# Two spacer tensors in SBUF grow by 32 bytes each, under the operands' high and low parts

## What is computed

```python
# first block
mod = silu(c) @ w_ada + b_ada                      # 1024 x 6144, one row
h = layer_norm(x) * (1 + sc1) + sh1
proj = h @ w_in                                    # gated conv (31 taps), pooling, two gates
mix = (sigmoid(gate_a) * ya + sigmoid(gate_b) * yb) @ w_out
x = layer_norm(ALPHA * x + g1 * mix)
up = causal_dwconv(h2 @ w_up, w_dw_f)              # 3 taps, 2 x 2816 channels
x = layer_norm(ALPHA * x + g2 * ((gelu(gt) * v) @ w_down))
# second block, layer 0: gated delta rule, 8 heads; layer 1: block attention, 8 heads
h = layer_norm_2(a * h + mixer(h))
h = layer_norm_2(a * h + (silu(h @ w1) * (h @ w3)) @ w2)   # 2816 channels, in both layers
```

## Time and profile before

| | us |
|---|---|
| median of three executions | 1171.5 |
| lowest, highest | 1166.29, 1176.5 |
| the profiled execution | 1169.08 |
| its span, from first to last instruction | 1167.3 |
| TensorE busy in it | 1109.0 |
| VectorE busy | 807.5 |
| ScalarE busy | 614.9 |

### The profile page before, as it was taken

The page is one execution under the profiler, slowest core; times in us unless marked ns, Lnnn a source line. Parts: engine busy times, 40 slices in busy tenths (PEclk is TensorE's granted clock), DMA queues, the critical chain, the costliest instruction groups (busy, mean ns, idle before and its releaser), DMA issues.

```text
span 1167.3 us, 20553 instructions
## 1 busy us (share of the span) xinstructions
PE 1109.0 (95%) x8544; PEld 1068.4 (92%) x8544; DVE 807.5 (69%) x1360; ACT 614.9 (53%) x1028; POOL 3.3 (0%) x13
## 2 busy tenths in 40 slices
PE   7998989999999998879989999999999999999997
PEld 7998878899999987679989999999999799999996
DVE  7988489877878787586666755555589656555555
ACT  5567444555555648742454554545455545545453
POOL 0000000000000000000000000000000000000000
PEclk9999999999999998989989999999999999999998
DMA  9985247257666523234224266565536332665620
GB/s 377 418 314 179 74 145 279 95 175 246 229 223 210 180 76 113 61 102 146 73 73 143 70 205 198 183 197 184 160 120 201 130 128 91 217 198 181 197 75 37
DMA packets 58557, 195.60 MB, mean 168 GB/s; under 512 B 10848, under 2 KB 11232, under 8 KB 58208
## 3 DMA queue, kind: packets, MB, share of 16 engines
q1 hardware_dynamic: 58464, 194.28, 49.1%
HBM read 192.94 MB, written 1.31 MB: 166 GB/s over the span
## 4 chain that ended last, share of the span: by engine, by line
PE 73%; DVE 17%; ACT 7%; issue 2%; SPq 1%; DMA 0%; POOL 0%; ACTq 0%; DVEq 0%; POOLq 0%
PE ps L512 61%; DVE lo L1475 4%; PE ps L725 3%; ACT hi L1008 2%; DVE raw L1462 2%; PE ps L610 2%; PE ps L519 2%; DVE B L1484 1%; PE ps L531 1%; DVE ev L1713 1%; DVE st L1492 1%; PE ps L507 1%; DVE ev L1710 1%; DVE B L1788 1%; DVE B L1497 1%
## 5 line engine op out<-in xcount | busy, mean ns | idle before, releaser
L512 PE MATMUL ps<-hh,hi 128*128 128x256 f32 x1792 | 511.2, 285 | 15.2 <-DVE hl L1509 3.5
L512 PE MATMUL ps<-hh,lo 128*128 128x256 f32 x1792 | 504.3, 281 | 0.0
L512 PE MATMUL ps<-hl,hi 128*128 128x256 f32 x1792 | 503.9, 281 | 0.0
L1475 DVE TENSOR_TENSOR lo<-raw,hi 128x1024 fp32r<-128x1024 f32 x311 | 378.2, 1222 | 171.9 <-ACT hi L1008 171.1
L512 PEld LDWEIGHTS ps<-hh,hi 128*128 128x128 f32 x1792 | 340.7, 190 | 19.9 <-issue 9.6
L1008 ACT ACTIVATE hi<-raw 128x1024 fp32r<-128x1024 f32 x311 | 324.2, 1051 | 51.9 <-PE ps L512 51.6
L512 PEld LDWEIGHTS ps<-hl,hi 128*128 128x128 f32 x1792 | 340.6, 190 | 1.1
L512 PEld LDWEIGHTS ps<-hh,lo 128*128 128x128 f32 x1792 | 340.7, 190 | 0.0
L512 PE MATMUL ps<-fh,hi 128*128 128x256 f32 x392 | 109.9, 280 | 3.9 <-ACT B L1112 2.9
L512 PE MATMUL ps<-fh,lo 128*128 128x256 f32 x392 | 108.8, 278 | 0.0
L512 PE MATMUL ps<-fl,hi 128*128 128x256 f32 x392 | 108.8, 277 | 0.0
(11 more groups left out here) (256 smaller groups left out, 1221.8 us busy)
## 6 DMA issues: line engine op xcount, KB each, us to landing
raw<-in_w SPq DMA_DIRECT2D x359, 512.0 KB, 4.2
B<-in_t SPq DMA_DIRECT2D x2, 512.0 KB, 4.8
xa<-in_x SPq DMA_DIRECT2D x1, 1024.0 KB, 10.4
B<-in_r SPq DMA_DIRECT2D x1, 1024.0 KB, 6.0
out<-h SPq DMA_DIRECT2D x4, 256.0 KB, 2.0
cst<-in_c SPq DMA_DIRECT2D x1, 864.0 KB, 8.3
B<-between SPq DMA_DIRECT2D x32, 4.0 KB, 1.6
vec<-in_v SPq DMA_DIRECT2D x1, 328.5 KB, 6.7
```

The costliest lines, as they stand in the source:

```text
L512: m = g.matmul(o, l, r, start=first and n == 0, stop=last and n == 2, skip_group_check=True)
L1475: g.tensor_tensor(lo[:, j % SPLIT, :], raw[:, PLACE[j] % RAW, :], hi[:, j % SPLIT, :].bitcast(F), ALU.subtract).then_inc(*up("lo", j))
```

## The change

The unused tensor `gap0` grows from 24 to 32 words per partition and `gap1` from 8 to 16. With that `hh` and `hl` start 32 bytes further on, and `fh`, `fl` and everything declared behind them 64 bytes further on. The distance from `hi` to `hh` becomes 42816 bytes (remainder 64), that from `hi` to `fh` 42816 + 16384 + 64 = 59264 bytes (remainder 128 when divided by 256, 0 when divided by 128). Nothing else differs.

```diff
         ones = sb("ones", [P, 3, P])
-        gap0 = sb("gap0", [P, 24])
+        gap0 = sb("gap0", [P, 32])
         hh = sb("hh", [P, NC, S], FR)
         hl = sb("hl", [P, NC, S], FR)
-        gap1 = sb("gap1", [P, 8])
+        gap1 = sb("gap1", [P, 16])
         fh = sb("fh", [P, 4, S], FR)
         fl = sb("fl", [P, 4, S], FR)
         idle = sb("idle", [P, S], FR)
```

## The result

The changed kernel takes 1178.75 us (median of 20 executions, 1174.12 to 1181.75), the kernel before 1171.35 (median of 20). The ratio is 1.0056, with a 95% interval of 1.0043 to 1.0069: slower by 0.56%, some 6.6 us. The forecast was 1163.5, a gain of 8; the measured median lies at the slow end of the stated range of 1148 to 1179. The profiled execution took 1178.45 us, 9.4 more than the profiled one of before; its span is 1176.7.

The account below looks back on a forecast made before the run. The prediction took TensorE's matmul step in L512 to bound the kernel. It summed -8.0 us for hh and 0 for everything else against 1169.1, giving 1161.1, or 1163.5 for the median, with a range of 1148 to 1179.

Parts of the forecast that it names:

- What bounds the kernel: TensorE's matmul step in L512, 61% of the chain; 0.82 of a saving there reaches the end.
- The step depends on the distance: Operand's address relative to the weights likely sets the matmul step: 119.5, 117.0 and 115.2 ns at 0, 32 and 64 bytes.
- hh at 64 takes fh's mixture of steps: All 5376 matmuls with hh go from 117.0 to 115.2 ns: -9.7 us, of which -8.0 us reaches the end.
- a sign of being wrong: Feed-forward networks: hh having the long step in all three would show the forecast wrong; long step 117.8 ns.
- the argument against the short step: In the undisturbed stretch from 327.88 us all of fh's runs had the long step, against hh locking into 113.3.
- The bound that the text did give for this case: All 5376 matmuls with hh in the long step, 117.8 against 117.0 ns: +0.8 ns each, +4.3 us.
- fh at 128 costs 0: The 1176 down-projection matmuls with fh: between -4.2 us (111.6 ns) and +5.1 us (119.5 ns), taken as 0.
- The trend 119.5, 117.0, 115.2: Matmul steps in ns read from the trace at 0 (idle), 32 (hh) and 64 bytes (fh, weighted mean).
- The flips and the rest: 456 flipped matmuls, 1.4 us either way, and everything behind fh moving by 64 bytes: both taken as 0.
- The slower rival: fh's 1176 down-projection matmuls back at distance 0, +5.1 us: 1176.6, or 1180.9 with hh in the long step; chance 0.19.
- Short step everywhere: hh locks into 113.3 ns (-16.3 us) and fh gets quicker still (-3.4 us): 1151.8; chance 0.27.
- Nothing moves: The matmul step belongs to something other than the distance, so the time stays at 1171.5; chance 0.14.

Follow-up runs that it names:

- both0: hh, hl, fh and fl all moved to distance 0, against the kernel before: ratio 1.0165 (1.0142 to 1.0189).
- micro_plain: Whole computation left out, only bare matmuls, 72 at each distance 0 to 248 bytes, with and without breaks: steps of 113.3 to 122.2 ns.
- hh64_only: Only hh and hl moved to 64 bytes, fh and fl kept at 64, against the kernel before: ratio 1.0025 (1.0001 to 1.0048).
- micro_far: Computation left out, bare matmuls at 32, 64, 112, 128 and 192 bytes plus 0, 256, 512 and 768: 112 always 113.3 ns, 128 at 118.6 to 118.8.
- micro_handover: Computation left out, TensorE alone: 48 matmuls at one distance, then 24 at another, from four starts; at (32, 64) the second took 117.9 or 113.7 ns.
- micro_traffic: Computation left out, bare matmuls at six distances in the kernel's weight layout, with ScalarE, VectorE, both or neither working: 113.3 ns at 112, 120.0 at 0.

## Why the prediction was wrong, point by point

**What bounds the kernel: right.** The bound is TensorE's step in L512, nothing else changed, and a dearer step reached the end. That 0.82 of it would count can't be checked to the digit, but both0, priced in the same way, came out at 1.0165 for 1.016.

**The step depends on the distance: right, by more than was known.** The inference from three rows was confirmed with bare matmuls, whose steps go from 113.3 to 122.2 ns in micro_plain with nothing but the distance changed.

**hh at 64 takes fh's mixture of steps, -1.8 ns: the step that failed.** It was wrong in sign: `hh` went from 117.1 to 117.8, +0.7 ns, which with the forecast's own 0.82 is +3.1 us in the place of -8.0. The forecast carried a mean of 115.2 from `fh` to `hh` as if the mixture belonged to the address. It hung on what ran before: `fh` at 64 had its short runs behind `hh` at 32. Nothing in the prediction asked what the new neighbour would do. With `hh` at 64 the short step goes from both, all but wholly, in all three networks, which the prediction itself named as a sign of being wrong: of the changed kernel's groups of twelve with `hh` only 4 of 378 are short. hh64_only shows the same in the second and third network, and TensorE alone does at (64, 64) as long as it isn't stopped. Why a run at 64 behind a run at 64 starts long and not short is open. The count itself, 26 of 44, was one draw; a second execution had 39. That also takes the ground from the argument against the short step, that the stretch from 327.88 held the long one: in the second execution all of fh's units there were short. The bound that the text did give for this case, +0.8 ns and +4.3 us, is the one that came true.

**fh at 128 costs 0: too low.** It was put at the middle of 111.6 and 119.5 and lies at 118.6, so +3.3 ns x 1176 = +3.9 us against a top end of +5.1. With +3.1 for `hh` that makes 7.0 us, for 6.6 measured. The low end came from a plain float32 row of 128 columns, which says nothing about a step with 256; the shortest step of this form seen in any loop is 113.3.

**The trend 119.5, 117.0, 115.2.** Three points of a jagged curve. With 24 at 120.0 and 40 at 119.3 between them, no line through 0, 32 and 64 means anything. (The 119.5 of the earlier trace rows is a stretch divided by its count; the usual step of `idle` in that trace is 120.0.)

**The flips and the rest: near enough at 0.** The flipped matmuls with `fh` went from 232.5 to 233.3 ns, 264 x 0.8 = 0.2 us.

**The slower rival.** With `fh` at 119.5 and `hh` in the long step it gave 1180.9; the measured 1178.75 is 2 us from it. It took both terms whole; with the 0.82 of the forecast's own sum they give 1179.2. Its price was right to 1 ns and its second half, the long step in `hh`, is what happened. Its reason was not: the pattern doesn't repeat after 128 bytes, since 112 and 240 differ (113.3 and 117.2 ns in micro_plain). "Short step everywhere", at 1151.8, didn't happen at 64; at distance 192 it did, in the second network wholly and over the profiled execution for two thirds of `hh`, with 1158.09 in the median. "Nothing moves" is out.

## What to carry to other kernels

In this case the place of the moving operand against the weights, modulo 256 bytes, was worth up to 8% of the step of float32r matmuls (the type of `hi`, `lo`, `hh` and the other parts) of 128 x 128 x 256: 113.3 against 122.2 ns in micro_plain. Where such matmuls bound a kernel, it costs a spacer tensor to try. A bare loop over distances shows which steps a distance can have; which of them the kernel gets, it must show itself. Compare the kernel's steps with the bare loop's before you read anything into a distance: two runs here had the steps of 128 (118.7 ns) where the sum of the sizes gave 112 (113.3). A step read at one address must not be carried to another operand when one address shows two steps: ask first what the run before it did, and take the bounds, not the mean. Two spacers moved together should be priced as a pair, since the first also set the step of the second operand in the networks.

## What the runs showed of the hardware that was not expected

- At the full granted clock (1.00) the step of a plain float32r matmul with 256 columns lay between 113.3 and 122.2 ns in micro_plain, by the distance between the weights' and the operand's starts: 120.0 at all of 8, 24, 88, 104, 168, 184 and 200 bytes, 113.3 at 112 and 192.
- The distances 64 and 192 each had two lasting steps, 113.3 and 117.8 ns, and 32 had 116.7 and 117.8 (micro_far). A series of hundreds of matmuls stayed in one of them (21 units with `fh` at 113.3 in the second network of before, 22 at 117.8 in hh64_only). 64 had another one behind a break (117.8) than without it (113.3, micro_plain), behind `idle`'s matmuls (117.9) than behind plain float32 ones (113.7, micro_handover), and behind an operand at 32 (113.7 in before) than behind one at 64 (117.8 in hh64_only).
- VectorE and ScalarE, each busy for 7.00 of 7.00 us, changed none of the steps at 0, 32, 64, 112 and 128 bytes in micro_traffic by 0.1 ns.
- A shift by 32 bytes of `raw` and everything declared behind it changed nothing that can be told (1.0003, 0.9985 to 1.0021).
